# Sums of squares of eight head norms: one plain fp32 product, or two rounded products over a high and a low part

## The chip, the core and the metric

The kernel runs on one core of a Trainium2 chip, in one launch. The metric is device time in microseconds; the kernel before takes 3092.11 us in the median of three runs. Below, TensorE, VectorE, ScalarE and GpSimd are PE, DVE, ACT and POOL in the rows.

## What is computed

Two transformer blocks for 1024 tokens of width 1024. The change is in the second block, in its latent attention. Four heads have a query and a key of 192 values each (128 without and 64 with rotary position), and each of these eight is normed over its 192 values before the scores. Cut to that:

```python
q_m = _rmsnorm(jnp.concatenate([q_nope, q_rope], axis=-1), mla_q_norm_w[layer])
k_m = _rmsnorm(jnp.concatenate([k_nope, k_rope], axis=-1), mla_k_norm_w[layer])
o_mla = _mla_attention(q_m, k_m, v_mla).reshape(b, s, MLA_WIDTH)

def _rmsnorm(x, w):
    x32 = x.astype(jnp.float32)
    y = x32 * lax.rsqrt(jnp.mean(x32 * x32, axis=-1, keepdims=True) + EPS)
    return (y * w.astype(jnp.float32)).astype(x.dtype)
```

Everything is fp32. The kernel makes most products from a high part (type fp32r, a rounded fp32 that TensorE takes in one pass) and a low part (the rest), three rounded products in place of one exact one.

## The kernel before

Activations lie transposed, features on the 128 partitions and the 1024 tokens along the free axis, so a sum over features is a TensorE product with a 128x128 matrix of ones, which also spreads the sum to all partitions. A norm of a head is made in stages, whose names stand in the kernel's one list of work `S`; every engine walks the same list and does its own part of each stage:

- `mn0`: ScalarE squares the 64 rotary rows into `mrt` and the 128 other rows into `sqn` (L1808 to L1812); VectorE adds the first to the second (L2423).
- `mn1`: TensorE multiplies `sqn` by the ones (L980, two column halves of 512) into a pair of PSUM banks `big`. In type fp32, unrounded.
- `mn2`: ScalarE makes the reciprocal root from that pair as Ln and Exp (`root`, L1424 and L1426) into `mrt`; VectorE scales the two parts of the head by it (L2436, L2440).
- `mn3`: ScalarE, VectorE and, for queries, GpSimd split the scaled head into high and low part (L1818 to L1824, L2445, L2447, L2566, L2569).

The buffers of the key of the first latent head are called `sqn_k` and `mrt_k`.

The attention of one head is cut into units of a query tile: scores (`sc`, L1117, into `big`), maximum over the scores (L2169), exponential (ScalarE, L1460), reciprocal and scaling (L2189, L2191), transposes of the probabilities (`pt`, L1140, into `tbank`), their eviction by ScalarE (`mpt`, `dpt`, L1412), and the product with the values (`pv`, L1158, into `obank`). The differential attention before it (names `dprob`, `dpt`) works alike with two maps a head. Units are strung together by `attend_pairs`, which puts the stages of the next head's norms between the units by two written tables, `early` (ahead of a unit's value product) and `late` (behind it). So the order within each engine is fixed when the kernel is built, and each engine's queue is run strictly in that order; waits between engines are semaphores. The norms of latent head 0 stand in the last units of the differential attention, those of heads 1 to 3 each in the eight units of the head before.

While the query's low part (`q_rope_lo`, `q_lo`) is made on GpSimd, key norms are under way.

Of the kernel before, what the change touches and what calls it, by code (L numbers as in the profile page):

```python
# [19 lines left out]
ALU = mybir.AluOpType  # L20
# [93 lines left out]
def _emit(nc, ctx, known, a):  # L114
# [17 lines left out]
    ident = at("ident_sb", M0 + 4096, [P, P])  # L132
    ones = at("ones_sb", M0 + 4608, [P, P])
    blocks = at("blocks_sb", M0 + 5120, [P, P])
# [92 lines left out]
    sqk, mrk = at("sqn_k", X0 + 16 * K, [P, T]), at("mrt_k", G2 + 8 * K, [P, T])  # L227
    norm_bufs = lambda which, h: (sqk, mrk) if (which, h) == ("k", 0) else (sqn[h], mrt[h])
    mvf = by_head("mv_f", R0, G1 + 36 * K)

# [87 lines left out]
    s_mm, s_msq = sig("max_prepared"), sig("head_squares")  # L318
    s_hn = sig("head_normed")
    s_mhi, s_mlq, s_mlk, s_mlo = sig("head_hi"), sig("query_lo"), sig("key_lo"), sig("query_rope_lo_placed")  # L320
    s_ptu = sig("pt_used")
# [321 lines left out]
    filler[24] = [("krope", "kr", ("tables", "b2"))]  # L643
    early[24] = [("cnorm", "cq0")]
    mnorms = [(q, h) for h in range(4) for q in "qk"]
    late = {25: [("cnorm", "cq1"), ("cnorm", "ckv")],
# [20 lines left out]
    for h in range(3):  # L667
        u = 8 * h
        late[u] = [("mh", h + 1)]
        late[u + 1] = [("v_t", f"mv{h + 1}"), ("mn0", "q", h + 1)]  # L670
        early[u + 3] = [("mn1", "q", h + 1), ("mn2", "q", h + 1)]
        early.setdefault(u + 4, []).extend([("mn0", "k", h + 1), ("mn3", "q", h + 1)])
        early[u + 5] = [("mn1", "k", h + 1), ("mn2", "k", h + 1)]
        late[u + 5] = [("mn3", "k", h + 1)]
    late[25] = [("y2split", 4), ("y2split", 5)]
    late[27] = [("y2split", 6), ("y2split", 7)]
# [182 lines left out]
    def ss_of(key):  # L859
        return nb_of(key)["ss"]  # L860
# [43 lines left out]
    def _(pe):  # L904
# [79 lines left out]
        def sum_of_squares(key):  # L984
            pe.wait_ge(*s_ss.at(key, DC - 2))
            full_product(("ss", key), s_arel, [(ones[:, :], ss_of(key)[:, :]), (ones[:, :], nb_of(key)["sq"][(DC - 1) % 2][:, :])],
                         ready=s_sq.at(key, DC - 1))
# [24 lines left out]
        for stage, *x in S:  # L1012
# [9 lines left out]
            elif stage == "lam":  # L1022
                pe.wait_ge(*s_mm.at("lamp"))
                out = take(("lam",), s_arel)
                pe.matmul(out[:, 0:2], ones[0:HD, :], lam_v[:, 4:6], start=True, stop=True).then_inc(*s_big.mark("lam"))
            elif stage == "xin":
# [9 lines left out]
            elif stage == "ss":  # L1036
# [5 lines left out]
                if key in ("q_a", "kv_a"):  # L1042
                    parts = (0, 1) if key == "q_a" else (2,)
                    for n in parts:
                        pe.wait_ge(*s_sq.at("c", n))
                    full_product(("ss", key), s_arel, [(ones[:, :], sqc[n][:, :]) for n in parts])
                    continue
                pe.wait_ge(*(s_ssd if key == "attn2" else s_ss).at(key, DC - 1))
                full_product(("ss", key), s_rel if key == "attn2" else s_arel, [(ones[:, :], ss_of(key)[:, :])])
            elif stage in ("rope", "lin"):  # L1050
# [290 lines left out]
            elif stage == "donorm":  # L1341
                h, = x
                pe.wait_ge(*s_msq.at("do", h))
                full_product(("donorm", h), s_arel, [(ones[:, :], out_norm(h)[0][:, :])])
            elif stage == "uqr":
# [3 lines left out]
            elif stage == "mh":  # L1349
                h, = x  # L1350
                q = [(P * k, clh[k][:, :], cll[k][:, :], None) for k in range(2)]
                kv = lambda n: [(P * (2 + n), clh[2][:, :], cll[2][:, :], s_nl.at("c", 2))]
                weight_job(f"mh{h}", ("mh", h, "q"), P, q, end=False)
                weight_job(f"mh{h}", ("mh", h, "k"), P, kv(0), end=False)
                weight_job(f"mh{h}", ("mh", h, "v"), P, kv(1))
            elif stage == "mn1":
                which, h = x
                pe.wait_ge(*s_mm.at("mn", which, h))
                full_product(("mn", which, h), s_arel, [(ones[:, :], norm_bufs(which, h)[0][:, :])])


    @block.scalar
    def _(act):
# [99 lines left out]
        for stage, *x in S:  # L1463
# [330 lines left out]
            elif stage == "mn0":  # L1794
# [14 lines left out]
                else:  # L1809
                    act.wait_ge(*(s_hn.at("mq", h) if h else s_rot.at("uqr", 0)))  # L1810
                    act.activation(mrz[0:HD, :], krb[0:HD, :], ACT.Square)
                act.activation(sqz[:, :], (qz if which == "q" else kz)[h][:, :], ACT.Square).then_inc(*s_msq.mark(which, h))  # L1812
            elif stage == "mn3":
                which, h = x
# [27 lines left out]
    def _(dve):  # L1842
# [85 lines left out]

        dve.memset(ones[:, :], 1.0)
        dve.memset(eps_c[:, :], EPS).then_inc(*s_mm.mark("ones"))  # L1930
        for stage, *x in S:
# [7 lines left out]
            elif stage == "biasrow":  # L1939
# [3 lines left out]
                for n in range(4):  # L1943
                    ins = dve.tensor_scalar(tabf[:, 2 * n:2 * n + 2], ones[0:HD, 0:2], tab[:, n:n + 1], 1.0 / ATTN_SCALE, ALU.mult, ALU.mult)
                step(ins, "tf")
# [470 lines left out]
            elif stage == "ksum" or (stage == "mn0" and x != ["k", 0]):  # L2416
# [5 lines left out]
                sqz, mrz = norm_bufs(which, h)  # L2422
                dve.tensor_tensor(sqz[rows, :], sqz[rows, :], mrz[rows, :], ALU.add).then_inc(*s_mm.mark("mn", which, h))  # L2423
            elif stage == "mn2":
                which, h = x
# [503 lines left out]
```

## Time and profile before

| | |
|---|---|
| three runs, us | 3091.37, 3092.11, 3097.47 |
| span of the profiled execution, us | 3087.7 |
| TensorE busy | 2937.6 us, 95% |
| VectorE busy | 1751.3 us, 57% |
| ScalarE busy | 1204.6 us, 39% |
| GpSimd busy | 1203.0 us, 39% |
| mean granted TensorE clock | 0.986 |
| latent attention with head norms, us from the start | about 2105 to 2300 |
| norms of latent head 0 | about 2074 to 2105 |

The profiled execution's own time is its span, 3087.7 us, and the few microseconds around it; the shortest of the runs is 3.7 us above that span, the median 4.4, the longest 9.8. The span runs from the first instruction to the last. A busy share says how full an engine is, not whether others wait for it. The granted clock is TensorE's share of full speed.

### The profile page before, as it was taken

How to read it: one execution, taken by the hardware profiler on the slowest of the kernel's cores; microseconds unless marked ns; L12 is line 12 of the kernel's file. 1: busy time of each engine (PE TensorE's matmuls, PEld its weight loads, DVE VectorE, ACT ScalarE, POOL GpSimd, SP SyncE). 2: the span in 40 equal slices, each digit the busy share in tenths (PEclk: the TensorE clock that was granted, in tenths of full speed). 3: DMA queues.
4: the chain of work that ended last, by engine and by line, in shares of the span. 5: the costliest groups of instructions: out<-in, count | busy, mean ns of one | idle time of the engine just before them, and what ended most of it. 6: DMA issues, size and time to landing. Idle time of an engine off the chain costs nothing. (4 is left out here: it accounts for less than half of the span.)

```text
span 3087.7 us, 36537 instructions
## 1 busy us (share of the span) xinstructions
PE 2937.6 (95%) x13886; PEld 2267.0 (73%) x13886; DVE 1751.3 (57%) x2645; ACT 1204.6 (39%) x1806; POOL 1203.0 (39%) x686
## 2 busy tenths in 40 slices
PE   7888998999999999999999899998999999999999
PEld 5656666666788788887887666656778788878887
DVE  5777775875232644445467555577552544455554
ACT  4445553555433433333124344456562322221110
POOL 5322334222244887774124101031103887722221
PEclk9999998999999999999999999999999999999999
DMA  7311212111251223334231311010003233342222
GB/s 199 71 49 48 62 49 55 42 56 55 85 188 48 68 83 86 84 86 137 67 102 43 114 34 38 17 41 18 11 4 109 83 109 109 109 163 95 95 75 75
DMA packets 279422, 236.36 MB, mean 77 GB/s; under 512 B 23860, under 2 KB 252084, under 8 KB 278708
## 3 DMA queue, kind: packets, MB, share of 16 engines
q1 hardware_dynamic: 279288, 234.65, 25.5%
q8 instruction: 75, 1.23, 0.2%
q14 instruction: 59, 0.48, 0.1%
HBM read 171.14 MB, written 53.51 MB: 73 GB/s over the span
## 5 line engine op out<-in xcount | busy, mean ns | idle before, releaser
L952 PE MATMUL big<-g_hi,w_hi 128*128 128x512 f32 x2112 | 688.5, 407 | 32.0 <-POOL w_lo L2458 6.7
L2458 POOL TENSOR_TENSOR w_lo<-w_raw,w_hi 128x1024 fp32r<-128x1024 f32 (+2 forms) x147 | 340.7, 2318 | 919.1 <-ACT w_hi L1375 919.1
L952 PE MATMUL big<-g_lo,w_hi 128*128 128x512 f32 x2112 | 660.0, 394 | 0.0
L952 PE MATMUL big<-g_hi,w_lo 128*128 128x512 f32 x2112 | 658.4, 393 | 0.0
L952 PEld LDWEIGHTS big<-g_hi,w_hi 128*128 128x128 f32 x2112 | 377.8, 190 | 191.2 <-issue 112.7
L952 PEld LDWEIGHTS big<-g_hi,w_lo 128*128 128x128 f32 x2112 | 399.7, 189 | 87.8
L952 PEld LDWEIGHTS big<-g_lo,w_hi 128*128 128x128 f32 x2112 | 398.9, 189 | 86.8
L1375 ACT ACTIVATE w_hi<-w_raw 128x1024 fp32r<-128x1024 f32 (+2 forms) x147 | 146.2, 995 | 417.1 <-PE big L952 402.7
L1403 ACT ACTIVATE a_hi<-a_raw 128x512 fp32r<-128x512 f32 x114 | 72.1, 632 | 332.9 <-POOL a_raw L2465 329.9
L1223 PE MATMUL big<-b_hi,a_hi 128*128 128x512 f32 x456 | 178.7, 392 | 7.9 <-DVE b_lo L2254 6.0
L1223 PE MATMUL big<-b_lo,a_hi 128*128 128x512 f32 x456 | 178.1, 391 | 0.0
L1223 PE MATMUL big<-b_hi,a_lo 128*128 128x512 f32 x456 | 178.0, 390 | 0.0
L2266 DVE TENSOR_TENSOR c<-c,big 128x512 f32<-128x512 f32 x114 | 78.3, 687 | 156.1 <-PE big L1223 154.7
L2473 POOL TENSOR_TENSOR a_lo<-a_raw,a_hi 128x512 fp32r<-128x512 f32 x114 | 153.4, 1346 | 31.9 <-ACT a_hi L1403 31.9
L2266 DVE TENSOR_TENSOR c<-c,obank 128x512 f32<-128x512 f32 x76 | 52.2, 687 | 188.4 <-ACT c L1646 178.9
L1412 ACT ACTIVATE pt<-tbank 128x512 f32<-128x512 f32 (+1 forms) x160 | 83.6, 553 | 182.4 <-PE tbank L1140 182.4
L2547 POOL TENSOR_TENSOR gst_b<-gst_b,r_rep 128x1024 f32<-128x1024 f32 x16 | 38.4, 2401 | 228.4 <-ACT gst_b L1486 228.4
L1223 PE MATMUL tbank<-b_hi,a_hi 128*128 128x512 f32 x304 | 120.0, 395 | 4.2 <-POOL a_lo L2473 4.2
L2100 DVE TENSOR_SCALAR_CACHE_REDUCE tally_a<-idx_acc,edge 128x384 f32<-128x384 f32 (+2 forms) x140 | 119.1, 850 | 4.8
L1223 PE MATMUL tbank<-b_lo,a_hi 128*128 128x512 f32 x304 | 119.0, 391 | 0.0
L1223 PE MATMUL tbank<-b_hi,a_lo 128*128 128x512 f32 x304 | 118.8, 391 | 0.0
L1223 PE MATMUL obank<-b_hi,a_hi 128*128 128x512 f32 x304 | 118.3, 389 | 0.0
(345 smaller groups left out, 5439.9 us busy)
## 6 DMA issues: line engine op xcount, KB each, us to landing
a_spill<-c SPq DMA_DIRECT2D x54, 512.0 KB, 3.4
g_lo<-a_spill SPq DMA_DIRECT2D x54, 512.0 KB, 5.1
w_raw<-in_w_in SPq DMA_DIRECT2D x51, 512.0 KB, 4.2
w_raw<-in_w_down SPq DMA_DIRECT2D x40, 512.0 KB, 4.3
w_raw<-in_w_up SPq DMA_DIRECT2D x27, 512.0 KB, 6.0
u_raw<-in_w_up SPq DMA_DIRECT2D x27, 512.0 KB, 5.9
rot<-rope_in SPq DMA_DIRECT2D x68, 128.0 KB, 2.3
g_spill<-gst_b SPq DMA_DIRECT2D x16, 512.0 KB, 3.0
```

Source lines behind the costliest of these rows:

```text
L952: ins = pe.matmul(out[0:m, HALF * h:HALF * h + HALF], w[slot][:, col:col + m], x[:, HALF * h:HALF * h + HALF], start=p == 0, stop=p == tot ...
L1223: ins = pe.matmul(banks[q], w[q][:, P * k:P * k + P], x[q][:, k, :], start=(k == 0 and z == 0), stop=(k == 3 and z == 2))
L1375: act.activation(w_hi[w % 2][:, 0:n], w_raw[w % 2][:, 0:n], ACT.Copy).then_inc(*s_whi.mark(w))
L1403: act.activation(ah[q][:, :], az[q][:, :] if src is None else src, ACT.Copy).then_inc(*s_ah.mark(stage, q, n))
L1412: act.activation(dest, src, ACT.Copy).then_inc(*s_te.mark(*key))
L2100: dve.tensor_scalar(tally, z, edge[:, i:i + 1], 0.0, ALU.is_ge, ALU.add, accum_out=above[:, i:i + 1]).then_inc(*s_tk.mark("count", bit, i))
L2266: dve.tensor_tensor(dest, one_, banks[other] if isinstance(other, int) else other, op).then_inc(*s_dr.mark(stage, m, what))
L2458: pool.tensor_tensor(w_lo[s][:, 0:n], w_raw[s][:, 0:n], w_hi[s][:, 0:n].bitcast(F32), ALU.subtract).then_inc(*s_wlo.mark(w))
L2473: pool.tensor_tensor(al[q][:, :], az[q][:, :] if src is None else src, ah[q][:, :].bitcast(F32), ALU.subtract).then_inc(*s_al.mark(stage, ...
L2547: pool.tensor_tensor(z[:, :], z[:, :], r_rep[:, :], ALU.mult).then_inc(*s_gt.mark(name))
```

## The change

The sum of squares of each of the eight norms is split like any other operand. A new stage `mnh` has ScalarE copy the sum of squares, rounded, into the high part (`mrt_hi`, which lies where `mrt` lies), and VectorE subtract that from the sum, in place, as the low part (`sqn_lo`). The product `mn1` then goes over both parts, each with the ones in type fp32r. The ones are written as fp32 and copied to fp32r at the start; other users read them through a cast. All else stays.

```diff
-    ones = at("ones_sb", M0 + 4608, [P, P])
+    ones_raw, ones_r = at("ones_raw", M0, [P, P]), at("ones_sb", M0 + 4608, [P, P], F32R)
...
+    sqn_lo, mrt_hi = by_head("sqn_lo", G2 + 44 * K, G1 + 52 * K, F32R), by_head("mrt_hi", G2 + 48 * K, G1 + 8 * K, F32R)
+    sqk_lo, mrk_hi = at("sqn_k_lo", X0 + 16 * K, [P, T], F32R), at("mrt_k_hi", G2 + 8 * K, [P, T], F32R)
+    norm_parts = lambda which, h: (sqk_lo, mrk_hi) if (which, h) == ("k", 0) else (sqn_lo[h], mrt_hi[h])
...
+    early[30] = [("mnh", "k", 0), ("mnh", "q", 0)]
...
+    for h in range(3):
+        late.setdefault(8 * h + 2, []).append(("mnh", "q", h + 1))
+        late.setdefault(8 * h + 4, []).append(("mnh", "k", h + 1))
...
             elif stage == "mn1":
                 which, h = x
-                pe.wait_ge(*s_mm.at("mn", which, h))
-                full_product(("mn", which, h), s_arel, [(ones[:, :], norm_bufs(which, h)[0][:, :])])
+                lo, hi = norm_parts(which, h)
+                pe.wait_ge(*s_sqh.at("mn", which, h))
+                full_product(("mn", which, h), s_arel, [(ones_r[:, :], hi[:, :]), (ones_r[:, :], lo[:, :])],
+                             ready=s_sql.at("mn", which, h))
...
+            elif stage == "mnh":
+                which, h = x
+                act.wait_ge(*s_mm.at("mn", which, h))
+                act.activation(norm_parts(which, h)[1][:, :], norm_bufs(which, h)[0][:, :], ACT.Copy).then_inc(*s_sqh.mark("mn", which, h))
...
-        dve.memset(ones[:, :], 1.0)
+        dve.memset(ones_raw[:, :], 1.0).then_inc(*s_mm.mark("ones_set"))
+        dve.wait_ge(*s_mm.at("ones_set"))
+        dve.tensor_copy(ones_r[:, :], ones_raw[:, :])
...
+            elif stage == "mnh":
+                which, h = x
+                lo, hi = norm_parts(which, h)
+                dve.wait_ge(*s_sqh.at("mn", which, h))
+                dve.tensor_tensor(lo[:, :], norm_bufs(which, h)[0][:, :], hi[:, :].bitcast(F32), ALU.subtract).then_inc(*s_sql.mark("mn", which, h))
```

Where the new stages come to stand in each queue, at three places. First ScalarE from the query norm of head 1 to the eviction behind its root; the buffer numbers differ by one or two between the kernels. Before:

```order
L1812 ACTIVATE sqn_215<-q_z_239 128x1024
L1412 ACTIVATE mpt_189<-tbank 128x512
L1412 ACTIVATE mpt_187<-tbank 128x512
L1460 ACTIVATE mprob_186,sm<-mprob_186,mn 128x1024 x2
L1412 ACTIVATE mpt_188<-tbank 128x512
L1412 ACTIVATE mpt_189<-tbank 128x512
L1783 ACTIVATE sq_o<-y_d 128x1024
L1424 ACTIVATE mrt_217<-big,eps_c 128x1024
```

And of the changed kernel:

```order
L1822 ACTIVATE sqn_216<-q_z_246 128x1024
L1422 ACTIVATE mpt_190<-tbank 128x512
L1422 ACTIVATE mpt_188<-tbank 128x512
L1470 ACTIVATE mprob_187,sm<-mprob_187,mn 128x1024 x2
L1422 ACTIVATE mpt_189<-tbank 128x512
L1422 ACTIVATE mpt_190<-tbank 128x512
L1793 ACTIVATE sq_o<-y_d 128x1024
L1826 ACTIVATE mrt_hi_228<-sqn_216 128x1024
L1434 ACTIVATE mrt_218<-big,eps_c 128x1024
```

The copy stands directly ahead of the root (L1424, now L1434). It is the same for all norms of heads 1 to 3; in heads 2 and 3 there is no `sq_o`. Between the squares and the root of a key norm stand the two splits of the query, an exponential, two evictions and in head 1 `sq_o`.

Second VectorE, from the sum of head 1's key norm on. Of before:

```order
L2423 TENSOR_TENSOR sqn_215<-sqn_215,mrt_217 64x1024
L2189 RECIPROCAL rc<-sm 128x1
L2191 TENSOR_SCALAR mprob_185<-mprob_185,rc 128x1024
L2169 TENSOR_SCALAR mprob_186,mn<-big 128x1024
L2414 SCALAR_TENSOR_TENSOR y_d<-y_d,gains,rt_o 128x1024
```

And of the changed kernel:

```order
L2439 TENSOR_TENSOR sqn_216<-sqn_216,mrt_218 64x1024
L2444 TENSOR_TENSOR sqn_lo_226<-sqn_216,mrt_hi_228 128x1024
L2205 RECIPROCAL rc<-sm 128x1
L2207 TENSOR_SCALAR mprob_186<-mprob_186,rc 128x1024
L2185 TENSOR_SCALAR mprob_187,mn<-big 128x1024
L2430 SCALAR_TENSOR_TENSOR y_d<-y_d,gains,rt_o 128x1024
```

The subtraction follows its sum at once and stands ahead of the unit's reciprocal, scaling and maximum. In query norms a unit's reciprocal, scaling and maximum stand between sum and subtraction.

Third, ScalarE at the norms of latent head 0, of the changed kernel; before, the rows were the same without the two with `mrt_k_hi` and `mrt_hi`:

```order
L1822 ACTIVATE sqn_215<-q_z_245 128x1024
L1826 ACTIVATE mrt_k_hi<-sqn_k 128x1024
L1826 ACTIVATE mrt_hi_227<-sqn_215 128x1024
L1422 ACTIVATE dpt_178<-tbank 128x512
L1422 ACTIVATE dpt_179<-tbank 128x512
L1470 ACTIVATE dprob_170,sm<-dprob_170,mn 128x1024
L1422 ACTIVATE dpt_180<-tbank 128x512
```

Here both copies stand ahead of two evictions. On VectorE both subtractions stand, behind the maxima of a unit, ahead of the reciprocal L2189. On TensorE the two rows `sqn` and `sqn_k` of 128x512 x2 become four, high ahead of low, in the same place.

## Rows read from the trace of the kernel before

**Rows 1.** Busy us (and instructions) by engine in 20 us of the latent attention

```profile
core 0: us, PE busy (x) PEld busy (x) DVE busy (x) ACT busy (x) POOL busy (x), PEclk, DMA share, GB/s
2185.00:2205.00 20.00, 19.50 (x92) 14.91 (x91) 13.21 (x20) 16.03 (x22) 5.19 (x2) 1.00 0.16 40
```

**Rows 2.** Chain that ended last: start, us, what; ten rounded score products

```profile
2127.23 2.29 PE big L1117 x10
```

**Rows 3.** Timeline (start, us, engine), query norm of head 1

```profile
2123.77 1.22 DVE L2423 TENSOR_TENSOR sqn<-sqn,mrt 64x1024 f32<-64x1024 f32 x1 [2.39 <-ACT sqn L1812]
...
2129.14 1.06 ACT L1412 ACTIVATE mpt<-tbank 128x512 f32<-128x512 f32 x2
...
2129.36 1.88 PE L980 MATMUL big<-sqn,ones_sb 128*128 128x512 f32 x4
...
2130.10 1.05 ACT L1783 ACTIVATE sq_o<-y_d 128x1024 f32<-128x1024 f32 x1
...
2131.08 1.89 PE L1158 MATMUL obank<-mpt,mv 128*128 128x256 f32 x8
```

**Rows 4.** Timeline, key norm of head 1

```profile
2142.10 1.22 DVE L2423 TENSOR_TENSOR sqn<-sqn,mrt 64x1024 f32<-64x1024 f32 x1 [3.59 <-ACT sqn L1812]
...
2143.37 1.98 PE L980 MATMUL big<-sqn,ones_sb 128*128 128x512 f32 x4 [0.61 <-DVE sqn L2423]
...
2145.72 2.84 POOL L2569 TENSOR_TENSOR q_lo<-q_z,q_hi 128x1024 fp32r<-128x1024 f32 x1
2145.89 1.99 PE L1158 MATMUL obank<-mpt,mv 128*128 128x256 f32 x8 [0.54 <-ACT mpt L1412]
...
2146.22 1.05 ACT L1783 ACTIVATE sq_o<-y_d 128x1024 f32<-128x1024 f32 x1
...
2147.16 1.11 ACT L1424 ACTIVATE mrt<-big,eps_c 128x1024 f32<-128x1024 f32 x1
...
2153.75 1.10 PE L1158 MATMUL obank<-mpt,mv 128*128 128x256 f32 x4 [0.97 <-ACT mpt L1412]
```

**Rows 5.** Timeline, query norm and key norm of head 2

```profile
2184.77 1.06 ACT L1412 ACTIVATE mpt<-tbank 128x512 f32<-128x512 f32 x2
...
2187.92 1.89 PE L1158 MATMUL obank<-mpt,mv 128*128 128x256 f32 x8
...
2197.94 1.05 ACT L1412 ACTIVATE mpt<-tbank 128x512 f32<-128x512 f32 x2
...
2198.74 2.62 POOL L2569 TENSOR_TENSOR q_lo<-q_z,q_hi 128x1024 fp32r<-128x1024 f32 x1
...
2199.69 1.11 ACT L1424 ACTIVATE mrt<-big,eps_c 128x1024 f32<-128x1024 f32 x1 [0.70 <-issue]
...
2206.13 1.10 PE L1158 MATMUL obank<-mpt,mv 128*128 128x256 f32 x4 [1.62 <-ACT mpt L1412]
```

**Rows 6.** Timeline, query norm and key norm of head 3

```profile
2237.13 1.07 ACT L1412 ACTIVATE mpt<-tbank 128x512 f32<-128x512 f32 x2
...
2239.89 1.89 PE L1158 MATMUL obank<-mpt,mv 128*128 128x256 f32 x8
...
2251.03 2.63 POOL L2569 TENSOR_TENSOR q_lo<-q_z,q_hi 128x1024 fp32r<-128x1024 f32 x1
...
2251.66 1.11 ACT L1424 ACTIVATE mrt<-big,eps_c 128x1024 f32<-128x1024 f32 x1 [0.30 <-issue]
```

**Rows 7.** Latent head 0: GpSimd and VectorE timelines; then one stretch, columns as rows 1

```profile
2101.06 3.14 POOL L2569 TENSOR_TENSOR q_lo<-q_z,q_hi 128x1024 fp32r<-128x1024 f32 x1
...
2101.92 3.36 DVE L2447 TENSOR_TENSOR k_lo<-k_z,k_hi 128x1024 fp32r<-128x1024 f32 x1
...
2105.00:2110.00 5.00, 4.46 (x13) 3.61 (x14) 0.85 (x3) 0.00 (x0) 0.00 (x0) 0.66 0.00 0
```

**Rows 8.** VectorE timeline, norms of latent head 0

```profile
2084.13 1.21 DVE L2423 TENSOR_TENSOR sqn<-sqn,mrt 64x1024 f32<-64x1024 f32 x1
...
2088.05 0.16 DVE L2189 RECIPROCAL rc<-sm 128x2 f32<-128x2 f32 x1
...
2091.06 0.17 DVE L2189 RECIPROCAL rc<-sm 128x2 f32<-128x2 f32 x1 [0.49 <-ACT dprob L1460]
```

More of the change, by code:

```diff
@@ L319, in _emit @@
     s_hn = sig("head_normed")
+    s_sqh, s_sql = sig("head_squares_hi"), sig("head_squares_lo")
     s_mhi, s_mlq, s_mlk, s_mlo = sig("head_hi"), sig("query_lo"), sig("key_lo"), sig("query_rope_lo_placed")
@@ L985, in sum_of_squares @@
             pe.wait_ge(*s_ss.at(key, DC - 2))
-            full_product(("ss", key), s_arel, [(ones[:, :], ss_of(key)[:, :]), (ones[:, :], nb_of(key)["sq"][(DC - 1) % 2][:, :])],
+            full_product(("ss", key), s_arel, [(ones_r[:, :].bitcast(F32), ss_of(key)[:, :]), (ones_r[:, :].bitcast(F32), nb_of(key)["sq"][(DC - 1) % 2][:, :])],
                          ready=s_sq.at(key, DC - 1))
@@ L1024, in _ @@
                 out = take(("lam",), s_arel)
-                pe.matmul(out[:, 0:2], ones[0:HD, :], lam_v[:, 4:6], start=True, stop=True).then_inc(*s_big.mark("lam"))
+                pe.matmul(out[:, 0:2], ones_r[0:HD, :].bitcast(F32), lam_v[:, 4:6], start=True, stop=True).then_inc(*s_big.mark("lam"))
             elif stage == "xin":
@@ L1045, in _ @@
                         pe.wait_ge(*s_sq.at("c", n))
-                    full_product(("ss", key), s_arel, [(ones[:, :], sqc[n][:, :]) for n in parts])
+                    full_product(("ss", key), s_arel, [(ones_r[:, :].bitcast(F32), sqc[n][:, :]) for n in parts])
                     continue
                 pe.wait_ge(*(s_ssd if key == "attn2" else s_ss).at(key, DC - 1))
-                full_product(("ss", key), s_rel if key == "attn2" else s_arel, [(ones[:, :], ss_of(key)[:, :])])
+                full_product(("ss", key), s_rel if key == "attn2" else s_arel, [(ones_r[:, :].bitcast(F32), ss_of(key)[:, :])])
             elif stage in ("rope", "lin"):
@@ L1343, in _ @@
                 pe.wait_ge(*s_msq.at("do", h))
-                full_product(("donorm", h), s_arel, [(ones[:, :], out_norm(h)[0][:, :])])
+                full_product(("donorm", h), s_arel, [(ones_r[:, :].bitcast(F32), out_norm(h)[0][:, :])])
             elif stage == "uqr":
@@ L1943, in _ @@
                 for n in range(4):
-                    ins = dve.tensor_scalar(tabf[:, 2 * n:2 * n + 2], ones[0:HD, 0:2], tab[:, n:n + 1], 1.0 / ATTN_SCALE, ALU.mult, ALU.mult)
+                    ins = dve.tensor_scalar(tabf[:, 2 * n:2 * n + 2], ones_r[0:HD, 0:2].bitcast(F32), tab[:, n:n + 1], 1.0 / ATTN_SCALE, ALU.mult, ALU.mult)
                 step(ins, "tf")
```

## The prediction

> **What bounds the kernel now.** I read first the busy time by stretches, then the chain of waits, and only then the order of time around each of the eight products that the change touches. In a typical 20 us of the latent attention TensorE works 19.50, VectorE 13.21 and ScalarE 16.03 [rows 1]. So TensorE sets the pace, and its own time there is worth its full length. But ScalarE is no idle neighbour: its queue is strict, and what stands in it at the wrong place arrives late. In the chain of waits ten rounded products of 512 columns take 2.29 us, 0.229 us each [rows 2]. The plain product of a norm takes 1.72 us, from its start at 2129.36 to the next TensorE row at 2131.08 [rows 3]: four records of 0.43 us (two matmuls, each recorded twice).
>
> The order of time shows the margins. Query norm of head 1: VectorE's sum ends at 2124.99, TensorE comes to the product only at 2129.36, and the next thing that it does is the value product at 2131.08 [rows 3]. Key norm of head 1: the sum ends at 2143.32, and TensorE has already waited 0.61 us for it [rows 4]. So the query norms have 4.4 us to spare and the key norms none.
>
> **What the change removes.** Each product becomes four rounded matmuls in place of two plain ones: 4 x 0.229 = 0.92 against 1.72 us, 0.80 us less, for eight norms 6.4 us [rows 2, 3]. Nothing else is removed. The constant of ones now takes a copy more at the start, on VectorE; TensorE waits there for the first input's DMA, so I cost it at nothing. Without that cover it would be one small copy of 128 columns, far under the 1.22 us of a 1024-column row [rows 3].
>
> **What it adds.** For each norm a ScalarE copy of 128x1024, 1.05 us as the square of the same shape [rows 3], and a VectorE subtraction of 1024 columns, 1.22 us as the sum's row [rows 3]. Eight of each are 8.4 and 9.8 us of engine time. Neither engine is full, so the busy time alone would cost little. What costs is where they stand. The order shows it: in ScalarE's queue the copy is the last thing ahead of the root (L1424) that reads the finished product. Everything that stood between the squares and the root is now ahead of it. TensorE may not start before that copy, nor do the second half before the subtraction. I follow each norm.
>
> Query, head 1 [rows 3]. The two evictions start at 2129.14, the output norm's square at 2130.10, the next ScalarE operation can start 0.95 later, 2131.06 (the spacing from 2129.14 to 2130.10). The copy ends 2132.11, the subtraction 1.22 later plus 0.04 of hand-over, 2133.37. TensorE does the high half meanwhile, and the low half from 2133.41 for 0.46. The value product starts at 2133.87 where it started at 2131.08: **+2.8 us**, in which the 0.80 saved is already inside. VectorE stands still before the subtraction, so reciprocal, scale and maximum behind it come after 2133.4 too. TensorE's transposes of the scaled row stand behind the value product's 1.89 us, so they still find it; the next late thing is the root, by the same 2.8 us.
>
> Queries, heads 2 and 3 [rows 5, 6]. There is no output-norm square here. Evictions from 2184.77: copy 2185.72 to 2186.77, subtraction to 2188.03, low half to 2188.53, against 2187.92: **+0.6 us**. Head 3, evictions from 2237.13: by the same steps 2240.89 against 2239.89: **+1.0 us**.
>
> Keys. Between sum and product ScalarE has two splits of the query, an exponential, two evictions and, in head 1, a square. Head 1 [rows 4]: the square starts at 2146.22, the copy runs 2147.17 to 2148.22, where TensorE has waited since 2142.76. GpSimd's subtraction of the query's low part runs 2145.72 to 2148.56 beside it. How long VectorE's subtraction then takes is the open price. Its two bounds: 1.22 us as if alone, and the case of the first latent head, where the key's subtraction took 3.36 us beside one of GpSimd that ended at 2104.20, and so ended 1.08 us after it [rows 7]. I take the second, since it is the same kind of pair: 2149.64. The product is complete 0.67 us later (0.04 hand-over, 0.23 spacing, 0.39 of the last matmul), 2150.31, and the root starts 2150.35 against 2147.16, +3.2; TensorE's value product starts 2150.14 against 2145.89, +4.25, of which the 0.97 us that it then waited for ScalarE takes a part back: 3.3. So **+3.3 us**. Head 2 [rows 5]: copy done 2199.94 by the spacing from its evictions, GpSimd ends 2201.36, subtraction 2202.44, root 2203.15 against 2199.69: **+3.4 us**. Head 3 [rows 6]: GpSimd ends 2253.66, subtraction 2254.74, root 2255.45 against 2251.66: **+3.7 us**. With the subtraction at 1.22 us these three would be 3.1, 2.2 and 2.6, together 2.5 us less.
>
> The Trainium skill, SBUF — State Buffer, section "Who interferes with whom", says that VectorE with two SBUF inputs and GpSimd use one port pair under an exclusive lock: who comes second stands until the first is done. By that rule the late subtraction would end a full 1.22 us after GpSimd, 0.4 us more over the three keys; a sharing of bandwidth would leave it cheaper. The trace agrees with the lock.
>
> First latent head [rows 8]. Both its copies stand ahead of two evictions: the second waits for the sum that ends at 2085.34, and ends at 2086.4, so the evictions slip by 2.7 us, but the transposes behind them are not what ends last. The two subtractions, 2.4 us, stand ahead of the reciprocal at 2088.05, and so of the scaling behind it. The second reciprocal, at 2091.06, had waited 0.49 us idle and can give that back: 2.4 - 0.5 = **+1.9 us**, and everything up to the first latent scores is chained to it. TensorE already waits there, so the 0.80 us twice saved is worth nothing.
>
> Sum of the waits: 1.9 + 2.8 + 0.6 + 1.0 + 3.3 + 3.4 + 3.7 = 16.7 us.
>
> **The clock.** After waits in the first latent head TensorE's granted clock was 0.66 in the next 5 us [rows 7]: 3.4 us at the lower level (1.2 GHz), which costs half of that, 1.7 us, where TensorE sets the pace. In head 1's key norm it would stand 5.5 us, longer than any wait of that stretch; I count one fall there, 1.7 us. Behind the keys of heads 2 and 3 a fall would be covered by the 1.62 us that TensorE waits for ScalarE anyway [rows 5], except 0.4 us for the low half. For these two and for head 1's query (2.7 us of waiting, then 0.9) I count 0.8 us together; bounds 0 and 4. Clock: +2.5 us.
>
> [...]
>
> Altogether 19.2, +19 us. The profiled execution's span is 3087.7; it becomes 3106.7. The median is 4.4 us above that span (other runs 3.7 to 9.8), so 3092.1 + 19 = **3111.1 us**.
>
> **The rivals.** (1) *It is faster*: the copy and the subtraction are done when TensorE arrives, and only the half-price product counts: 0.80 x 6 = 4.8 us in the part that TensorE bounds, 6.4 at most, 3085.7 to 3087.3. For it: the queries have 4.4 us, the two operations take 2.3. Against it: the order puts evictions between. It decides at a copy that starts by 2127.1 in the query norm of head 1, and for key norms at a sum 2.3 us earlier than it is, which no row offers. Chance 0.02. (2) *The gain and the waits cancel*: if ScalarE took the copy as soon as the sum is there, the bill would be 3 x -0.8 for the queries, +0.2 for head 1's key (sum at 2143.32, then 1.05 + 1.22 + 0.46 = 2146.1 where 2145.89 stood), +1.9 in the first latent head: -0.3, 3091.8 us. The order speaks against it; chance 0.03. (3) *The waits are partly absorbed*: the delays of a query norm push its head's ScalarE work into later gaps, or a key's delay hides in the next one: half the sum, +7 to +13, 3099 to 3105. For it: VectorE and ScalarE have a third to a fifth of their time free [rows 1]. Against it: TensorE has only 0.97 and 1.62 us of waits to give behind each key. Chance 0.12. (4) *More falls of the clock or another queue late*: +25 to +35, 3117 to 3127. For it: VectorE stands still up to 5 us with the softmax row behind it. Chance 0.10. My case, +13 to +25, has 0.73.
>
> **The numbers.** My case's own range is 3105 to 3117. The range that leaves out at most 2 in 10: 3102 to 3119; its low end takes in the uncontended subtraction (-2.5), no fall of the clock (-2.5) and part of rival 3, its high end the falls at every wait and the spread of the median. A difference under 0.2% (6 us) is about what a measurement of this kernel can't tell from none: faster 0.02, same 0.04, slower 0.94.
>
> **What will show it.** The product's rows: four at 0.23 us spacing, with an idle time of about 2.7 (query 1), 0.6 (query 2), 0.9, and about 5.5, 2.3 and 1.6 us (keys) ahead of the high half, released by the ScalarE copy, and one ahead of the low half, released by the VectorE subtraction. The subtraction of keys longer than 1.22 us, ending 1.1 us after GpSimd's. The first latent scores 1.9 us later, the last ones about 18 us later than before, all else unmoved. A granted clock under 1 behind the key of head 1. I am wrong if the copy starts well before the evictions are done, if the next head's products come at an unshifted distance, or if something outside the latent attention moved by more than 2 us.

## The result and the profile after

The changed kernel takes 3113.07 us (median of 6 runs, 3110.16 to 3117.85), the kernel before 3091.74 on the same chip (6 runs, 3085.65 to 3097.47). The ratio is 1.007, with a 95% interval of 1.0055 to 1.0084: some 21 us slower, forecast was +19. The profiled span is 3108.0 us against 3087.7. Medians and ratios, here and below, leave out single executions that ran far slower with the same kernel.

The timeline of the changed kernel at the query norm of head 1, which answers to [rows 3]. Columns: start, duration, engine, line, operation, out<-in, shape, count, and in brackets the idle time of the engine before the row and who ended it.

```profile
2131.00 1.05 ACT L1826 ACTIVATE mrt_hi<-sqn 128x1024 fp32r<-128x1024 f32 x1
...
2132.09 1.23 DVE L2444 TENSOR_TENSOR sqn_lo<-sqn,mrt_hi 128x1024 fp32r<-128x1024 f32 x1 [4.17 <-ACT mrt_hi L1826]
2132.11 0.73 PE L988 MATMUL big<-mrt_hi,ones_sb 128*128 128x512 f32 x2 [2.60 <-ACT mrt_hi L1826]
...
2133.37 1.22 PE L988 MATMUL big<-sqn_lo,ones_sb 128*128 128x512 f32 x2 [0.53 <-DVE sqn_lo L2444]
...
2134.38 2.99 PE L1166 MATMUL obank<-mpt,mv 128*128 128x256 f32 x8
2134.67 1.11 ACT L1434 ACTIVATE mrt<-big,eps_c 128x1024 f32<-128x1024 f32 x1 [2.62 <-issue]
```

TensorE stands 2.60 us until ScalarE's copy and 0.53 us until VectorE's subtraction. Before, the product began without a wait. After the wait it is slow as well: the low half takes 1.22 us where the high half, just before, took 0.73, and the eight value matmuls 2.99 where they took 1.89 [rows 3]. The same place at the key norm of head 1 (against [rows 4]):

```profile
2150.11 2.35 POOL L2590 TENSOR_TENSOR q_lo<-q_z,q_hi 128x1024 fp32r<-128x1024 f32 x1
...
2151.57 1.05 ACT L1826 ACTIVATE mrt_hi<-sqn 128x1024 fp32r<-128x1024 f32 x1
2152.65 1.22 DVE L2444 TENSOR_TENSOR sqn_lo<-sqn,mrt_hi 128x1024 fp32r<-128x1024 f32 x1 [4.93 <-ACT mrt_hi L1826]
2152.67 1.22 PE L988 MATMUL big<-mrt_hi,ones_sb 128*128 128x512 f32 x2 [5.50 <-ACT mrt_hi L1826]
...
2153.93 1.22 PE L988 MATMUL big<-sqn_lo,ones_sb 128*128 128x512 f32 x2
```

And at the key norm of head 2 (against [rows 5]):

```profile
2207.86 2.35 POOL L2590 TENSOR_TENSOR q_lo<-q_z,q_hi 128x1024 fp32r<-128x1024 f32 x1
2208.02 1.05 ACT L1826 ACTIVATE mrt_hi<-sqn 128x1024 fp32r<-128x1024 f32 x1
...
2209.10 2.20 DVE L2444 TENSOR_TENSOR sqn_lo<-sqn,mrt_hi 128x1024 fp32r<-128x1024 f32 x1 [3.62 <-ACT mrt_hi L1826]
2209.12 0.73 PE L988 MATMUL big<-mrt_hi,ones_sb 128*128 128x512 f32 x2 [2.13 <-ACT mrt_hi L1826]
...
2211.35 0.94 PE L988 MATMUL big<-sqn_lo,ones_sb 128*128 128x512 f32 x2 [1.50 <-DVE sqn_lo L2444]
```

Two things differ between the keys. In head 1 GpSimd's subtraction ended at 2152.46, before VectorE's began, and that one took 1.22 us. In head 2 GpSimd's ended at 2210.21 and VectorE's, begun 1.1 us before that, took 2.20 and ended at 2211.30, 1.09 us behind it.

The granted clock (the column PEclk; at 1 it is 2.4 GHz, at half of it 1.2) in stretches of 5 us of the changed kernel:

```profile
core 0: us, PE busy (x) PEld busy (x) DVE busy (x) ACT busy (x) POOL busy (x), PEclk, DMA share, GB/s
2080.00:2085.00 5.00, 1.07 (x8) 0.85 (x8) 4.86 (x9) 2.96 (x5) 0.00 (x0) 0.70 0.00 2
2085.00:2090.00 5.00, 4.81 (x18) 4.05 (x19) 4.89 (x10) 3.65 (x8) 0.00 (x0) 0.62 0.02 3
...
2130.00:2135.00 5.00, 2.37 (x6) 1.65 (x7) 2.88 (x4) 2.38 (x4) 0.00 (x0) 0.82 0.00 0
2135.00:2140.00 5.00, 5.00 (x25) 4.15 (x24) 3.34 (x7) 3.95 (x6) 0.00 (x0) 0.84 0.00 0
2150.00:2155.00 5.00, 2.29 (x5) 1.38 (x6) 2.31 (x4) 2.62 (x4) 2.35 (x1) 0.53 0.60 157
```

Falls stand behind the waits of the first head, of head 1's query and of head 1's key, and behind the keys of heads 2 and 3:

```profile
2210.00:2215.00 5.00, 3.65 (x9) 2.96 (x10) 3.65 (x6) 2.58 (x3) 0.21 (x1) 0.67 0.38 106
2265.00:2270.00 5.00, 2.78 (x6) 1.79 (x7) 3.80 (x4) 1.48 (x3) 2.20 (x1) 0.63 0.24 52
```

Before, the only stretch of these 200 us under full clock was the one of [rows 7].

**Where the 21 us are.** Both kernels give TensorE the same number of matmul records, 13886, in the same order (a plain matmul leaves two records, as two rounded ones do); only in experiment 7 below are some of them in another order, since a key's product stands a unit later there. So the start of the same row can be compared in two traces, and the difference grows only where time is lost. The growth across each norm, in us, is the *step* of that norm; a negative step means that time is gained. For the changed kernel: first head 3.2, then query 4.5, key 4.0 (head 1), 0.7, 3.6 (head 2), 1.1, 4.2 (head 3), together 21.3. Behind the last norm the difference stays at 18.0 for 60 us (it was -3.3 ahead of the first one), and later it moves by 2.3 us with falls of the clock at places that both kernels have; that makes the 20.3 us between the two spans.

### The profile page after: what moved, and what is told of

It is laid out like the page before. It is cut to its first block and busy times, and to the rows that moved or that the text cites. A ratio compares the mean times of both kernels' runs of the same rounds, so it can differ in the third digit from the quotient of the medians.

```text
span 3108.0 us, 36554 instructions
## 1 busy us (share of the span) xinstructions
PE 2939.9 (95%) x13886; PEld 2271.7 (73%) x13886; DVE 1764.4 (57%) x2654; ACT 1212.0 (39%) x1814; POOL 1202.1 (39%) x686
```

## The experiments

All times are compared with the kernel before on the same chip; its medians beside them were 3092.9, 3092.3 and 3091.6 us. The table has the steps, read as above, beside what was timed. Column head 0 ends at the first latent scores (2105.5 us before), and *behind* is what the difference moves from there to 2128 us. Sums are taken before rounding. A step comes from one traced run of each kernel, a ratio from all of its runs. Line numbers of an experiment's rows differ by a few from those of the changed kernel.

```
                          head 0  behind   q1    k1    q2    k2    q3    k3    sum   ratio to before (95%)
changed kernel              3.2    0.0    4.5   4.0   0.7   3.6   1.1   4.2   21.3   1.0070 (1.0055 to 1.0084)
1 rounded squares           0.0    0.0   -0.8   0.0  -0.8  -0.8  -0.8  -0.4   -3.5   0.9982 (0.9971 to 0.9993)
2 plain behind split        4.0   -0.2    7.0   5.8   2.0   5.8   4.1   5.4   34.0   1.0129 (1.0111 to 1.0147)
3 product not behind split  3.9   -0.3    1.9   3.0   0.0   4.3   0.1   3.2   16.1   1.0045 (1.0032 to 1.0059)
4 queries early             2.4   -0.1   -0.8   3.6  -0.8   3.8  -0.8   3.7   11.1   1.0031 (1.0022 to 1.0041)
5 no subtraction            2.2   -0.1    2.1   3.5   0.0   2.5   0.3   2.0   12.4   1.0044 (1.0028 to 1.0060)
6 subtraction behind row    3.9   -0.2    0.0   3.6   0.2   5.5   0.2   5.8   19.1   1.0063 (1.0047 to 1.0078)
7 keys a unit later         0.6   -1.6   -0.8   8.7  -0.8   6.7  -0.8   6.9   19.0   1.0062 (1.0045 to 1.0079)
8 keys ahead of exponential 0.6    1.1   -0.8   2.2  -0.8   1.8  -0.8   1.9    5.1   1.0015 (1.0003 to 1.0028)
9 queries alone             0.6    1.1   -0.8   0.0  -0.8   0.0  -0.8   0.0   -0.7   0.9990 (0.9980 to 1.0000)
```

No work of the change stands in *behind*: it is the clock. All kernels wait there for the first latent head's low key, and what the clock does next differs. The kernel before has 0.66 in 2105 to 2110 us and 1.00 in the next 5 us; 7 has 1.00 in both; 9, whose head 0 is as plain as before, has this:

```profile
2105.00:2110.00 5.00, 4.00 (x10) 3.16 (x11) 1.07 (x2) 0.00 (x0) 0.00 (x0) 0.52 0.00 0
2110.00:2115.00 5.00, 5.00 (x19) 4.06 (x18) 2.90 (x5) 2.20 (x3) 0.70 (x1) 0.80 0.00 0
```

So the loss up to 2128 us lies between -1.0 and +1.6 us in three kernels that split nothing there (7, 8 and 9), and a figure for the first head is no surer than that. Behind it, places with equal code agree within about half a microsecond.

The theory at the start was that of the prediction: the operations themselves cost little; what costs is their place in two strict queues, and TensorE, which waits for them.

**1. The product's price alone.** No copy, no subtraction, one rounded sum passed over twice.

```diff
-                act.activation(sqz[:, :], (qz if which == "q" else kz)[h][:, :], ACT.Square).then_inc(...)
+                act.activation(norm_parts(which, h)[0][:, :], (qz if which == "q" else kz)[h][:, :], ACT.Square).then_inc(...)
...
+                lo = norm_parts(which, h)[0]
+                dve.tensor_tensor(lo[rows, :], lo[rows, :].bitcast(F32), mrz[rows, :], ALU.add).then_inc(...)
...
+                full_product(("mn", which, h), s_arel, [(ones_r[:, :], lo[:, :]), (ones_r[:, :], lo[:, :])])
```

> What it changes: no copy and no subtraction at all; ScalarE writes the head norms' squares rounded, VectorE's sum of them is written rounded too, and the product is two rounded passes over that one sum (both the same, so the sum is twice too large and less exact). It keeps the halved price of the product and removes everything that the change added beside it. Theory (the cost is the place of the copy and the subtraction in two strict queues): the gain of the product alone is left, 0.80 us for each of the six norms that TensorE's own time bounds, 4.8 us, up to 6.4: 3085.3 to 3086.9 against 3091.7 before. Query product starts without a wait, key product with the 0.6 us wait of before. Rival (rounded passes or rounded writes bring a cost of their own, in the clock or in the writing): 3091.7 or more.

Measured: 3087.48 us (12 runs), ratio 0.9982. Query norm of head 1 in its timeline:

```profile
2130.70 1.07 PE L988 MATMUL big<-sqn_lo,ones_sb 128*128 128x512 f32 x4
...
2131.60 1.89 PE L1166 MATMUL obank<-mpt,mv 128*128 128x256 f32 x8
```

From the product to the value product it is 0.90 us where it was 1.72 [rows 3]. The queries gain 0.8 us each, the keys 0.0, 0.8 and 0.4. So the halved price is real and worth 3.5 us by the trace, 5.4 by the medians; the loss of the changed kernel is the split's doing.

**2. Plain product behind the split.**

```diff
-                full_product(("mn", which, h), s_arel, [(ones_r[:, :], hi[:, :]), (ones_r[:, :], lo[:, :])],
-                             ready=s_sql.at("mn", which, h))
+                pe.wait_ge(*s_sql.at("mn", which, h))
+                full_product(("mn", which, h), s_arel, [(ones_r[:, :].bitcast(F32), hi[:, :].bitcast(F32))])
```

> What it changes: copy, subtraction and both waits stay, but the product is one plain fp32 pass over the high part alone, and starts only when the subtraction is done (the low part is left out of the sum). Theory: TensorE waits as long as in the changed kernel, and then spends 1.72 us where it had 0.46 left; 1.26 us for each of six norms, 7.6 us, and up to 2.5 more in the first head: 3120.6 to 3123.2. Rival (the clock, which falls after the waits, decides, not the path): a longer and denser product spares falls, 3113 or less. Rival (the product is hidden behind ScalarE's or VectorE's delay): 3113, no change.

Measured: 3133.5 us (three runs: 3123.7, 3133.5, 3134.5), ratio 1.0129, and steps of 34.0 against 21.3: 12.7 us more by the trace, where 7.6 to 10.1 were expected. The traced run is the shortest; by the medians it is 20 us more, and what the other two runs lost beside that has no trace. TensorE's time is on the path; that it would be hidden, or that a denser product would save falls of the clock, is refuted. Part of the excess is the clock. At head 1's query (7.0 against 4.5) the stretch behind the wait:

```profile
2137.17 3.75 PE L988 MATMUL big<-mrt_hi,ones_sb 128*128 128x512 f32 x4 [3.93 <-issue]
```

Its windows:

```profile
2135.00:2140.00 5.00, 2.83 (x4) 1.31 (x5) 3.19 (x5) 0.81 (x1) 0.00 (x0) 0.60 0.00 0
```

The plain product, 1.88 us long before the change, takes 3.75 there.

**3. The product not behind the split.** Copy and subtraction stand where they stood, the product is plain again and waits for the sum alone, the root waits for the subtraction.

```diff
-                pe.wait_ge(*s_sqh.at("mn", which, h))
-                full_product(("mn", which, h), s_arel, [(ones_r[:, :], hi[:, :]), (ones_r[:, :], lo[:, :])],
-                             ready=s_sql.at("mn", which, h))
+                pe.wait_ge(*s_mm.at("mn", which, h))
+                full_product(("mn", which, h), s_arel, [(ones_r[:, :].bitcast(F32), norm_bufs(which, h)[0][:, :])])
...
-                      [s_hn.at(*(("m" + mnorms[n - 1][0], mnorms[n - 1][1])))] if n > 1 else [])
+                      ([s_hn.at(*(("m" + mnorms[n - 1][0], mnorms[n - 1][1])))] if n > 1 else []) + [s_sql.at("mn", which, h)])
```

> What it changes: copy and subtraction are made at the same places in the same queues, but the product is again one plain pass over the sum and waits only for the sum, as before the change; the root waits for the subtraction, so that it cannot come earlier than the low part is there. TensorE's own wait is gone, the work of the other two engines and the late root are left. Theory (TensorE's wait in front of its next value product is what costs): the queries' three waits are gone (4.4 us), of the keys most of 10.4, and the falls of the clock with them, while the first head keeps its 1.9 to 3.3: 3094 to 3101. Rival (the late root and the late softmax row behind it are what costs, whoever waits): 3108 to 3118, TensorE then waits a little later for ScalarE.

Measured: 3107.2 us, ratio 1.0045. That is some 14 us over before, above what the theory gave (3094 to 3101) and just under the rival (3108 to 3118). It was run once more for its trace (ratio then 1.0051, 1.0034 to 1.0068):

> The same kernel as the one before it whose product does not stand behind the split (plain product over the sum, copy and subtraction in place, root behind the subtraction), for its trace. That one was timed at 1.0045 of the kernel before, between the two theories. Theory now: the queries' norms step by about 0 (TensorE goes on to its value product and transposes, the late root meets nothing), and what is left sits at the first head (about 2 us) and at the three keys, 3 us each, since there the copy and the subtraction also hold back the reciprocal and the scaling of the softmax row, which TensorE's transposes wait for. Rival: the queries too keep 1 us or more each.

The queries of heads 2 and 3 step by 0 and the keys by 3.0, 4.3 and 3.2, as expected; head 1's query keeps 1.9. Its timeline at the key norm of head 1:

```profile
2151.05 1.23 DVE L2442 TENSOR_TENSOR mrt_hi<-sqn,mrt_hi 128x1024 fp32r<-128x1024 f32 x1 [4.93 <-ACT mrt_hi L1824]
2152.19 0.16 DVE L2203 RECIPROCAL rc<-sm 128x1 f32<-128x1 f32 x1
2152.39 0.75 DVE L2205 TENSOR_SCALAR mprob<-mprob,rc 128x1024 f32<-128x1024 f32 x1
...
2153.24 1.59 PE L1148 MATMUL tbank<-ident_sb,mprob 128*128 128x128 f32 x8 [2.55 <-DVE mprob L2205]
```

TensorE no longer waits at the product, but its next transposes wait 2.55 us for a softmax row that VectorE could have scaled long ago: VectorE stood 4.93 us for ScalarE's copy with reciprocal and scaling queued behind the subtraction. So the first form of the theory falls. Taking away TensorE's own standing in front of the product gives back 5 of 21 us, although the plain product costs its old 0.8 us more at each norm again; a second chain through VectorE, nearly as long, holds most of the time.

**4. Only the queries' split moved**, to the head of its unit in both queues.

```diff
-        late.setdefault(8 * h + 2, []).append(("mnh", "q", h + 1))
+        early.setdefault(8 * h + 2, []).append(("mnh", "q", h + 1))
```

> What it changes: only the copy and the subtraction of the three later queries move, in both queues, from behind the unit's other work to ahead of it; in ScalarE's queue the copy then stands between the unit's two exponentials, ahead of the evictions, and in VectorE's the subtraction ahead of the reciprocal. Theory (place): the query sums are there 4.4 us ahead of TensorE, so the three waits go (2.8, 0.6, 1.0) and the product's saving is kept, with about 1 us of clock: 7 to 8 us less than 3113.1, less 1 if the exponential behind the copy is waited for: 3105 to 3107. Rival (it is the added engine work, not its place): 3111 to 3115, the wait turns up elsewhere, at the value product that waits for the second exponential.

Measured: 3103.56 us (10 runs), ratio 1.0031, half the loss gone by one word. By the steps 10.2 us came back, 8.7 of them at the three queries, where 7 to 8 were expected: the first query's step alone went from 4.5 to -0.8. The other 1.5 us are differences at the first head and the keys, whose code is the same in both. The granted clock of 2130 to 2140 us is 1.00 again in this trace. Head 1's query:

```profile
2133.01 0.62 PE L988 MATMUL big<-mrt_hi,ones_sb 128*128 128x512 f32 x2
2133.46 0.62 PE L988 MATMUL big<-sqn_lo,ones_sb 128*128 128x512 f32 x2
2133.91 1.89 PE L1166 MATMUL obank<-mpt,mv 128*128 128x256 f32 x8
```

No wait, 0.90 us for the product, and three steps of -0.8. The same copy and the same subtraction are made; that it is their engine time that costs is refuted for the queries.

**5. No subtraction.** The copy stays in place, the product passes over the high part twice.

```diff
-                full_product(("mn", which, h), s_arel, [(ones_r[:, :], hi[:, :]), (ones_r[:, :], lo[:, :])],
-                             ready=s_sql.at("mn", which, h))
+                full_product(("mn", which, h), s_arel, [(ones_r[:, :], hi[:, :]), (ones_r[:, :], hi[:, :])])
```

> What it leaves out: the low part; no subtraction is made, and the product is two rounded passes over the high part (it is counted twice). The copy stays in its place and TensorE waits for it. Theory (two waits in a row, each worth its own length): a query and the key of head 1 lose 0.80 us each (four matmuls after the copy take 0.96 us, where subtraction and low half took 1.76), the keys of heads 2 and 3, whose subtractions ran 2.2 us beside GpSimd, 1.8 each, and the first head 2.4 to 3.3: 9.2 to 10.1 us less than 3113.1, so 3103 to 3104, with some 11 us left to the copy's place alone. Rival (VectorE's subtraction, its contention with GpSimd and the softmax row behind it are most of the bill): 3098 or less. Rival (only the copy counts, the subtraction is hidden): 3110 or more.

Measured: ratio 1.0044, steps of 12.4, that is 8.9 us less than the changed kernel, where 9.2 to 10.1 were expected. The median of 8 runs, 3107.89 (3098.0 to 3112.91), is higher than that would give; the interval reaches from +9 to +19 us and does not decide between the two. By the trace the copy's place alone is worth 12 us, the subtraction 9.

**6. The second chain removed as well.** As 3, with VectorE's subtraction a stage of its own (`mnl`) behind reciprocal, scaling and maximum.

```diff
+        early[8 * h + 3].insert(0, ("mnl", "q", h + 1))
+        early[8 * h + 5].insert(0, ("mnl", "k", h + 1))
...
-            elif stage == "mnh":
+            elif stage == "mnl":
```

> What it changes: as the kernel whose product does not stand behind the split (plain product over the sum, copy in place, root behind the subtraction), but VectorE makes the subtraction behind reciprocal, scaling, maximum and output-norm scaling of its unit, not ahead of them. That one kept 16 of 21 us with TensorE's own wait gone, and its trace shows TensorE waiting for the scaled row instead. Theory (a second chain of almost the same length: copy, subtraction, reciprocal, scaling, TensorE's transposes): with it gone too the first query's 1.9 us go to 0, and of the keys' 3.0, 4.3 and 3.2 us 1 to 2 each stay, since the root, and the exponential behind it in ScalarE's queue, come 1 us later still; first head as before: 3098 to 3102. Rival (ScalarE's late root is what costs, not the row): 3107 or more.

Measured: 3110.62 us, ratio 1.0063. The expectation failed; the rival, the late root, has the number. The steps say where: head 1's query fell from 1.9 to 0, as the theory has it, but the keys rose from 3.0, 4.3 and 3.2 to 3.6, 5.5 and 5.8. Key norm of head 2:

```profile
2208.94 2.24 DVE L2444 TENSOR_TENSOR mrt_hi<-sqn,mrt_hi 128x1024 fp32r<-128x1024 f32 x1
...
2211.30 1.12 ACT L1434 ACTIVATE mrt<-big,eps_c 128x1024 f32<-128x1024 f32 x1 [2.63 <-DVE mrt_hi L2444]
...
2217.01 1.06 ACT L1422 ACTIVATE mpt<-tbank 128x512 f32<-128x512 f32 x2
...
2217.74 2.04 PE L1168 MATMUL obank<-mpt,mv 128*128 128x256 f32 x4 [5.11 <-ACT mpt L1422]
```

The transposes find their row, but ScalarE stands 2.63 us in front of the root with the exponential, both key splits and the evictions queued behind it, and TensorE meets that delay some 6 us later, as 5.11 us in front of a value product. Three chains run from the late copy to TensorE (product, scaled row, root). Taking one away, or two, gives almost nothing for a key. How long the third is by itself is not shown: the edit put its subtraction behind the row and so lengthened it, and no run leaves the root free of the subtraction with the other two chains gone.

**7. The keys' split, product and root a unit later**; queries as in 4; the first head's two norms plain, with no split.

```diff
-        early[u + 5] = [("mn1", "k", h + 1), ("mn2", "k", h + 1)]
-        late[u + 5] = [("mn3", "k", h + 1)]
+        early[u + 6] = early.get(u + 6, []) + [("mn1", "k", h + 1), ("mn2", "k", h + 1)]
+        late[u + 6] = [("mn3", "k", h + 1)]
...
-        late.setdefault(8 * h + 4, []).append(("mnh", "k", h + 1))
+        early.setdefault(8 * h + 5, []).append(("mnh", "k", h + 1))
...
+                if h == 0:
+                    pe.wait_ge(*s_mm.at("mn", which, h))
+                    full_product(("mn", which, h), s_arel, [(ones_r[:, :].bitcast(F32), norm_bufs(which, h)[0][:, :])])
+                    continue
```

> What it changes: the first head's two products are plain again, without copy and subtraction; the queries' copy and subtraction stand ahead of their unit's other work as in the kernel with the queries moved; the keys' copy and subtraction stand at the head of the unit after their sum, and product, root and scaling one unit later. Theory (place alone decides): no wait is left, the first head costs 0 and the six other norms save 0.80 us each: 4.8 us under before, about 3087 to 3088, ratio 0.998. Rival (a new wait: the output norm's row or the next head's low key, which now come a unit later): 3092 to 3098, with a wait at the first scores of heads 1 to 3 or at the transposes of the units concerned. Rival (the added engine time itself costs): above 3098.

Measured: 3110.60 us, ratio 1.0062. The expectation of 3087 failed. No product waits for the split, but the next head's first scores wait for its low key:

```profile
2158.18 1.28 DVE L2460 SCALAR_TENSOR_TENSOR k_rope<-kr_b,gains,mrt 128x1024 f32<-128x1024 f32 x1 [4.21 <-ACT mrt L1439]
...
2163.83 0.77 PE L1124 MATMUL big<-k_hi,q_hi 128*128 128x512 f32 x1 [5.96 <-DVE k_lo L2471]
```

The rival of a new wait was right in its place and far too low in its price (5 to 11 us in all): 8.7, 6.7 and 6.9 us at the three keys. The number lies with the last rival, added engine time (above 3098), but experiment 8, with the same operations in another place, is 14 us shorter. A key norm has no room on either side: its sum comes as TensorE arrives, its result is needed a unit later.

**8. The keys' copy right behind the sum, ahead of the exponential**, product and root where they were; otherwise as 7.

```diff
-        late.setdefault(8 * h + 4, []).append(("mnh", "k", h + 1))
+        early.setdefault(8 * h + 4, []).append(("mnh", "k", h + 1))
```

> What it changes: as the last one, but the keys' product, root and scaling stay where they were, and only copy and subtraction move, to right behind the key's sum, ahead of the exponential. Theory (place): the copy is done 2.3 us after the sum starts waiting for nothing, but the exponential and the two evictions come 1.05 us later each, and the subtraction runs beside GpSimd's: +1 to +2 us for each key, -0.8 for each query, first head 0: 3092 - 2.4 + 3 to 6, so 3093 to 3096. Rival (the keys' cost is engine time, not place): as with the queries moved and the first head's 3 us gone, 3100. Rival (it hides): 3087.

Measured: 3096.34 us (12 runs), ratio 1.0015. As expected: keys 2.2, 1.8, 1.9, queries -0.8; only the first head, which has no split, is 1.6 us off in this trace. All of the change's work for heads 1 to 3 is done here, and the loss of these six norms is 3.5 us where it was 18.1. At the first key:

```profile
2146.13 1.45 DVE L2447 TENSOR_TENSOR sqn_lo<-sqn,mrt_hi 128x1024 fp32r<-128x1024 f32 x1 [1.89 <-ACT mrt_hi L1829]
2146.15 1.17 PE L987 MATMUL big<-mrt_hi,ones_sb 128*128 128x512 f32 x2 [2.46 <-ACT mrt_hi L1829]
...
2146.65 3.17 POOL L2593 TENSOR_TENSOR q_lo<-q_z,q_hi 128x1024 fp32r<-128x1024 f32 x1
...
2147.69 2.67 DVE L2210 TENSOR_SCALAR mprob<-mprob,rc 128x1024 f32<-128x1024 f32 x1
```

**9. The queries of heads 1 to 3 alone in two rounded passes**, with the early place of 4; keys and first head plain. The edit is shown against 8.

```diff
-                if h == 0:
+                if h == 0 or which == "k":
...
-        early.setdefault(8 * h + 4, []).append(("mnh", "k", h + 1))
```

> What it changes: only the three later queries' products are made in two rounded passes, with copy and subtraction at the head of their unit; the first head's two norms and the three keys' have the plain product, with no copy and no subtraction. Theory (each norm is worth what its own place allows): three steps of -0.80 us, 0 everywhere else, 2.4 us under before: 3089.9 against 3092.3, ratio 0.9992; the step is seen in the trace, the median can hardly tell it. Rival (the trace's steps are partly given back behind): 3092 or more.

Measured: 3089.38 us (12 runs) against 3091.63, ratio 0.9990, interval 0.9980 to 1.0000. The steps of the norms are those expected, three of -0.8 and zeros at the keys. At the first head, which runs no split, 0.6 is a longer wait for the low key (2.98 us against 2.42), whose cause was not looked for, and 1.1 the clock behind it, shown above; so the trace as a whole has 0.7 us of the 2.4 left. By the medians this version is 2 us ahead of the kernel before, at the edge of what can be measured, and 24 us ahead of the changed one.

## Why the prediction was right, and where not

- **The sum.** 16.7 us of waits and 2.5 of clock were forecast, 19.2; the steps add to 21.3 and the ratio to 21.6. 3111.1 us was forecast, 3113.07 measured. That they agree so well is in part luck: the first head and head 1's query cost 3.0 us more than their terms, and head 1's key, with the 1.7 us of clock put there, 1.0 less.
- **The product, -0.80 each.** Right: 0.90 us against 1.72, shown by 1, 4 and 9. At the keys it is worth less, 0.0, 0.8 and 0.4 us in 1, and at the first head nothing, as forecast.
- **The copy last in ScalarE's queue, so that TensorE waits.** Right: waits of 2.60, 0.46, 0.85 us (queries; forecast 2.7, 0.6, 0.9) and 5.50, 2.13, 2.52 (keys; 5.5, 2.3, 1.6), all ended by the copy. Five are within 0.2 us; at head 3's key TensorE waits 0.9 us longer than forecast, for which no cause was looked for.
- **Query terms +2.8, +0.6, +1.0.** Steps 4.5, 0.7, 1.1. The later two are right. The first is mis-sized by 1.7 us, which is a fall of the clock: 0.82 and 0.84 in the two stretches behind it. With the wait gone (4) the clock stays at 1 there and the whole 4.5 + 0.8 comes back.
- **Key terms +3.3, +3.4, +3.7.** Steps 4.0, 3.6, 4.2. The contended price of the subtraction was right for heads 2 and 3 (2.20 and 2.12 us, ending 1.09 and 1.08 behind GpSimd; forecast 1.08) and wrong for head 1, where it ran uncontended at 1.22; there the clock took the difference, since both halves of the product needed 1.22 us for 0.73.
- **First head +1.9.** This step failed in its path, and by 1.3 us in size, of which the clock's own spread there (see the table) may be a part. The prediction let the evictions slip by 2.7 us and said that they do not end last, and charged VectorE's subtractions ahead of the reciprocal. The trace after has the slip at TensorE: the value product waits 3.15 us for its eviction, and the product, and the root behind it (idle 0.39 us until the product), come later for it, with the clock at 0.70 and 0.62:

```profile
2085.19 2.04 PE L1166 MATMUL obank<-dpt,dv 128*128 128x256 f32 x4 [3.15 <-ACT dpt L1422]
...
2090.85 1.12 ACT L1434 ACTIVATE mrt<-big,eps_c 128x1024 f32<-128x1024 f32 x1 [0.39 <-PE big L988]
```

Without any subtraction (5) 2.2 of the 3.2 us stay, which points at the copies' place for most of it; but 4, with copies and subtractions as in the changed kernel, has 2.4 there, so how the two divide is not shown.
- **The clock, +2.5.** The mechanism was right, the count too low: falls behind five norms, not one. What they cost cannot be separated everywhere; what the steps have over the forecast waits is 4.6 us, and of that the query's 1.7 is shown. The one fall that was counted, 1.7 us behind the key of head 1, is there (0.53 and 0.79), but all that this step has over its forecast wait is 0.7.
- **"So they still find it"** (TensorE's transposes and the scaled row, head 1's query). True in the changed kernel, but only since TensorE is itself late. Experiment 3 shows the row as a chain of its own. So the bill was right, and its reason, TensorE waiting at the product, was one of several.
- **The sign outside.** The prediction called itself wrong if something outside the latent attention moved by more than 2 us. Ahead of the first norm TensorE is 3.3 us earlier than before, and behind the last one the difference moves by 2.3. Kernels that are the same up to the first norm differ as much there (last section), and behind the last norm the kernel of 1 moves by 2.8, so this sign was set too tight; it does not tell against the mechanism.
- **The rivals.** Absorption of half (rival 3) did not come; each step is there in full, and the difference stays flat behind the last norm. More falls (rival 4) came in part.

What stays open: how the 4.6 us over the forecast waits divide between clock and small slips at each key, and why the runs of 2 and 5 lie above their traces.

## What to carry to other kernels

An operand split for cheaper matmul passes adds a copy on one engine and a subtraction on another, and both are worth their place, not their length: the same two operations cost 4.5 us ahead of the root and won 0.8 us one unit's work earlier. Before adding them, read for each product how long its input is ready before TensorE comes (4.4 us at the queries, nothing at the keys), and split only where that is more than the two operations take. When a late operation feeds several queues, undoing one wait shows little, because the next chain of nearly equal length takes its place; move the source, not the waits.

## What the runs showed that was not expected

- **The scaling of the softmax row collides with GpSimd as well.** In 8 the row `mprob<-mprob,rc` took 2.67 us (0.75 in 3) and ended at 2150.36, 0.54 us behind GpSimd's subtraction, which itself took 3.17 us where it takes 2.35 in the changed kernel; VectorE's own subtraction ahead of it, which overlapped the end of GpSimd's first one, took 1.45. So both sides pay, and an earlier split of a key moves the collision on to what follows it in VectorE's queue. The prediction had counted it for the subtraction alone. The Trainium skill, SBUF — State Buffer, section "Who interferes with whom", names this kind too (a one-input operation of VectorE may run in a mode that uses two ports, and then takes the shared pair); that the two collide, the trace bears out with these rows.
- **Equal code, unequal clock.** Ahead of the first norm all these kernels are the same but for the ones at the start, yet their TensorE rows at 2080 us lie between 3.3 us earlier and 3.2 later than before's. Two kernels that differ by under 5 us are better told apart by the steps across the changed place than by the spans.
